# Gating unit's u half: the high and low halves of the input as one moving operand of 512 columns, with the two partial results added ahead of the Gelu

## The reference, cut to what matters

```python
def chunked_sgu_mixer(x, w_in, ln_g, ln_b, w_s, b_s, w_out):
    z = jax.nn.gelu(x @ w_in, approximate=False)
    u, v = jnp.split(z, 2, axis=-1)
    v = layer_norm(v, ln_g, ln_b)
    v = v.reshape(B, n_chunks, SGU_CHUNK, SGU_GROUPS, SGU_GROUP_DIM)
    w = jnp.where(causal[None], w_s, jnp.zeros_like(w_s))
    mixed = jnp.einsum('gts,bnsgc->bntgc', w, v) + b_s.T[None, None, :, :, None]
    return (u * mixed.reshape(B, S, SGU_HALF)) @ w_out
```

## Time and profile before

| | |
|---|---|
| median of 3 runs | 1461.29 us |
| lowest, highest | 1460.56, 1461.58 us |
| span of the profiled execution (first to last instruction) | 1459.1 us |
| mean granted TensorE clock | 0.997 |
| TensorE busy | 1440.9 us (99%) |
| VectorE busy | 1087.9 us (75%) |
| ScalarE busy | 688.2 us (47%) |
| GpSimd busy | 206.9 us (14%) |

### The profile page before, as it was taken

How to read it: one execution, slowest core, us unless ns; L and a number is a source line. 1 busy time by engine, 2 the same in 40 slices (tenths; PEclk the granted TensorE clock), 3 DMA queues, 4 the chain that set the end, 5 groups by cost and what they waited for, 6 DMA issues and landing times.

```text
span 1459.1 us, 20805 instructions
## 1 busy us (share of the span) xinstructions
PE 1440.9 (99%) x7452; PEld 1215.4 (83%) x7452; DVE 1087.9 (75%) x1825; ACT 688.2 (47%) x854; POOL 206.9 (14%) x190
## 2 busy tenths in 40 slices
PE   9999999999999999999999999999999999999997
PEld 7988897888888888889988888898888897788886
DVE  5765757888778877757758877777877777688876
ACT  6346456444444444454435444465444477444442
POOL 1073111200001000300032000301000325510001
PEclk9999999999999999999999999999999999999999
DMA  8754653855656556566567556576556450465561
GB/s 276 233 170 151 198 172 125 301 178 187 212 185 208 172 191 211 173 207 198 170 205 238 173 194 208 172 244 219 173 190 212 147 178 30 136 238 174 181 212 67
DMA packets 198734, 273.96 MB, mean 188 GB/s; under 512 B 9617, under 2 KB 158225, under 8 KB 198418
## 3 DMA queue, kind: packets, MB, share of 16 engines
q1 hardware_dynamic: 194162, 256.10, 53.2%
q0 software_dynamic: 4368, 16.78, 3.3%
q10 hardware_dynamic: 144, 0.26, 0.0%
HBM read 271.80 MB, written 1.31 MB: 187 GB/s over the span
## 4 chain that ended last, share of the span: by engine, by line
PE 90%; DVE 3%; POOL 3%; ACT 2%; issue 1%; DMA 0%; SPq 0%; DVEq 0%; ACTq 0%; POOLq 0%
PE ps L665 26%; PE ps L667 25%; PE ps L666 25%; PE ps L777 3%; PE ps L760 3%; PE ps L771 3%; PE ps L706 1%; POOL wlo L2792 1%; ACT whi L1443 1%; PE ps L1151 0%; PE ps L1279 0%; DVE big L2616 0%; DMA raw<-in_w_in 0%; DVE wlo L2014 0%; POOL big L2838 0%
## 5 line engine op out<-in xcount | busy, mean ns | idle before, releaser
L2014 DVE TENSOR_TENSOR wlo<-raw,whi 128x2048 fp32r<-128x2048 f32 (+1 forms) x222 | 504.6, 2290 | 167.5 <-ACT whi L1443 165.5
L1443 ACT CAST whi<-raw 128x2048 fp32r<-128x2048 f32 (+1 forms) x237 | 449.0, 1894 | 372.5 <-PE ps L667 327.4
L665 PE MATMUL ps<-whi,st_hi 128*128 128x512 f32 (+1 forms) x1064 | 414.7, 390 | 0.0
L667 PE MATMUL ps<-whi,st_lo 128*128 128x512 f32 (+1 forms) x1064 | 412.5, 388 | 0.0
L666 PE MATMUL ps<-wlo,st_hi 128*128 128x512 f32 (+1 forms) x1064 | 412.3, 388 | 0.0
L2428 DVE STREAM_TRANSPOSE hidT<-hidden 32x128 f32<-32x128 f32 x800 | 242.3, 303 | 12.3
L667 PEld LDWEIGHTS ps<-whi,st_lo 128*128 128x128 f32 (+1 forms) x1064 | 198.8, 187 | 41.0
L665 PEld LDWEIGHTS ps<-whi,st_hi 128*128 128x128 f32 (+1 forms) x1064 | 198.9, 187 | 40.7 <-issue 0.3
L666 PEld LDWEIGHTS ps<-wlo,st_hi 128*128 128x128 f32 (+1 forms) x1064 | 198.9, 187 | 40.2
L665 PE MATMUL ps<-whi,hid_hi 128*128 128x512 f32 x400 | 156.2, 391 | 0.0
L667 PE MATMUL ps<-whi,hid_lo 128*128 128x512 f32 x400 | 155.7, 389 | 0.0
(11 more groups left out here) (267 smaller groups left out, 1431.9 us busy)
## 6 DMA issues: line engine op xcount, KB each, us to landing
raw<-in_ffn_w SPq DMA_DIRECT2D x260, 512.0 KB, 4.8
raw<-in_w_gate_up SPq DMA_DIRECT2D x44, 512.0 KB, 4.8
raw<-in_w_in SPq DMA_DIRECT2D x32, 512.0 KB, 5.2
raw<-in_sgu_w_in SPq DMA_DIRECT2D x32, 512.0 KB, 4.7
raw<-in_w_down SPq DMA_DIRECT2D x22, 512.0 KB, 5.2
raw<-in_sgu_w_out SPq DMA_DIRECT2D x16, 512.0 KB, 4.7
raw<-in_kv_w SPq DMA_DIRECT2D x12, 512.0 KB, 4.6
raw<-in_w_proj_attn SPq DMA_DIRECT2D x8, 512.0 KB, 4.3
```

The lines of the kernel that those rows point to most:

```text
L665: pe.matmul(o, a[0], b[0], start=start, stop=False)
L667: return pe.matmul(o, a[1], b[0], start=False, stop=stop)
L1443: act.copy(whi[:, s, 0:n], raw_unit(u, s, n)).then_inc(whi_ready, 1)
L2014: dve.tensor_tensor(wlo[:, s, 0:n], raw_unit(u, s, n), whi[:, s, 0:n].bitcast(F32), ALU.subtract).then_inc(wlo_ready, 1)
```

## The change

`st_hi` and `st_lo` become two halves of one tensor. For each unit and each block t of 128 features there is a bank of its own. The high weights are multiplied with both halves at once (two runs of 256 columns, 512 columns in all) into the two halves of the bank; the low weights are multiplied with the high input into the left half. So the left half holds high by high plus low by high, the right half high by low. ScalarE copies the right half to SBUF, VectorE adds the left half to it into `zu`, and the Gelu then works in place on `zu`. In the last of the 8 tiles the order of the two matmuls is turned. Banks are 6 and 7 for even n, 0 and 2 for odd n. VectorE's sum of unit n stands behind the low part of unit n + 2, and the sum of unit 0 ahead of `norm_v(1)`. `features` and `product` stay as they are for all other stages.

```diff
-        st_hi = sb("st_hi", [P, 16, S], F32R)
-        st_lo = sb("st_lo", [P, 16, S], F32R)
+        st_both = sb("st_both", [P, 2, 16, S], F32R)
+        st_hi, st_lo = st_both[:, 0, :, :], st_both[:, 1, :, :]
...
+        u_part = tmp[:, :, 512:512 + S]
...
-            plan(("sgu", j), 6 + n % 2, unit=first["sgu"] + n)
+            plan(("sgu", j, 0), (6, 0)[n % 2])
+            plan(("sgu", j, 1), (7, 2)[n % 2], unit=first["sgu"] + n)
...
-                key = ("sgu", j)
-                room(key)
-                features(first["sgu"] + n, [(0, bank(key)[:, 0:S]), (P, bank(key)[:, S:2 * S])]).then_inc(w_used, 1)
+                w_hi, w_lo = weights(first["sgu"] + n, KD, 256)
+                for t in range(2):
+                    key = ("sgu", j, t)
+                    room(key)
+                    both = bank(key).rearrange("p (x t) -> p x t", x=2)
+                    for k in range(KD):
+                        def high():
+                            return pe.matmul(both, w_hi[:, k, t * P:t * P + P], st_both[:, :, k, :], start=k == 0,
+                                             stop=k == KD - 1)
+                        if k < KD - 1:
+                            high()
+                        pe.matmul(both[:, 0, :], w_lo[:, k, t * P:t * P + P], st_hi[:, k, :], start=False, stop=False)
+                        if k == KD - 1:
+                            mm = high()
+                    if t == 0:
+                        mm.then_inc(*is_full(key))
+                    else:
+                        mm.then_inc(w_used, 1)
...
+            def u_low(n):
+                j = SGU_ORDER[n]
+                for t in range(2):
+                    act.wait_ge(*full(("sgu", j, t)))
+                    if n:
+                        act.wait_ge(u_ready, n)
+                    act.copy(u_part[:, t, :], bank(("sgu", j, t))[:, S:2 * S]).then_inc(u_low_copied, 1)
+
+            def u_gelu(n):
+                j = SGU_ORDER[n]
+                for t in range(2):
+                    act.wait_ge(*read(("sgu", j, t)))
+                z = zu[:, 2 * j:2 * j + 2, :].rearrange("p a b -> p (a b)")
+                act.activation(z, z, ACT.Gelu).then_inc(u_ready, 1)
+
             for n, j in enumerate(SGU_ORDER):
                 beside(first["sgu"] + n)
-                act.wait_ge(*full(("sgu", j)))
-                act.activation(zu[:, 2 * j:2 * j + 2, :].rearrange("p a b -> p (a b)"), bank(("sgu", j)),
-                               ACT.Gelu).then_inc(*is_read(("sgu", j)))
+                u_low(n)
+                u_gelu(n)
...
-                dve.wait_ge(*read(("sgu", j)))
+                dve.wait_ge(u_ready, n + 1)
...
+            def u_sum(n):
+                j = SGU_ORDER[n]
+                for t in range(2):
+                    dve.wait_ge(u_low_copied, 2 * n + t + 1)
+                    key = ("sgu", j, t)
+                    dve.tensor_tensor(zu[:, 2 * j + t, :], bank(key)[:, 0:S], u_part[:, t, :],
+                                      ALU.add).then_inc(*is_read(key))
+
             norm_v(0)
             beside(first["sgu"])
+            u_sum(0)
             norm_v(1)
             for n in range(1, 5):
                 beside(first["sgu"] + n)
+                u_sum(n)
             um_mix(0)
             um_mix(1)
             beside(first["sgu"] + 5)
+            u_sum(5)
             um_low(0)
             um_low(1)
...
```

More of the change, by code:

```diff
@@ L239, in build @@
         ws_masked = sem("ws_masked")
+        u_low_copied = sem("u_low_copied")
+        u_ready = sem("u_ready")
         u_mixed = sem("u_mixed")
@@ L2531, in _ @@
             beside(first["sgu"] + 6)
+            u_sum(6)
             um_low(2)
@@ L2536, in _ @@
             beside(first["sgu"] + 7)
+            u_sum(7)
             um_mix(6)
```

## The result

The changed kernel takes 1468.61 us (median of five runs, 1466.37 to 1468.96), against 1461.58 for the kernel before in the same comparison (1460.56 to 1463.33). The ratio is 1.0037, 95% interval 1.0026 to 1.0048: slower by 0.37%, outside the stated range and on the other side of it. Like start against like start gives 1.0036 and 1.0037.)

What follows compares the result with a forecast made beforehand. TensorE, busy 99% of the span, was taken as the bound. Units 44.38, mixes 7.09 and stall 1.39 gave 52.86 us against 53.17, 0.31 less: 1461.0 us forecast from a median of 1461.29, range 1459.5 to 1463.0.

Steps and rivals of the forecast that it cites:

- hand-over chain: ScalarE waits for VectorE's sum before Gelu and next rounding; all in time after unit 3, output matmul with 1.3 us slack.
- The clock: TensorE's granted clock: a stall of about 1.4 us should not lower it from 1.00.
- first stall: TensorE's new wait ahead of unit 3, forecast at 1.39 us where before there was none.
- The stall ahead of unit 3: TensorE waits until VectorE's sum 1 frees unit 3's bank: 1.39 us, unit 3 starting at 678.43.
- The direct gain: TensorE: three matmuls become two, 0.3600 to 0.3467 us, 128 times: 1.71 us saved, a unit 5.547 us.
- The two-run operand: The wide matmul reads two runs of 256 columns; no extra cost taken, a fresh start would be 0.0133 us each.
- the slow rate: Rival: each wide matmul takes 0.44 us in place of 0.227, 1486.9 us in all; chance 0.06.
- The additions and copies: Added per unit: two VectorE additions at 0.35 us and two ScalarE copies at 0.28, neither on the end's path.
- signs of being wrong: In the changed kernel's stage: a unit of 5.76 us or more, no wait at unit 3, or another wait besides.
- the second wait: Sign against the forecast: a TensorE wait besides the only one expected, about 1.4 us ahead of unit 3.
- The rivals: Four other outcomes: stall does not bite (0.12), fixed part remains (0.18), fast rate lost (0.06), handover dearer (0.10).
- The handover case: Rival: further waits at units 4 and the mixes of bank 3, mostly 1461.5 to 1463.5 us; chance 0.10.
- chance of 0.09 for slower: Whole kernel slower by over 0.2% (2.9 us): 0.06 for the lost fast rate plus 0.03 for dearer handover.

Runs made afterwards that it cites:

- e1_banks: The changed kernel with odd units in banks 4 and 5 and the mixes in 0, 2, 1, 3; 1463.29 us, ratio 1.000 to the kernel before.
- e3_filled: The changed kernel with four unneeded matmuls of constants in TensorE's wait ahead of the output matmul; 1465.43 us, ratio 1.0026 to the kernel before.

## Why the prediction was wrong, point by point

**The step that failed** is in the hand-over chain: "By the same pitches all arrives in time for the output matmul". It followed the data (the low products, the low weights) to that point and left out the third thing a matmul needs, its PSUM bank. The banks of units 3 and 4 and of the mixes had been walked through; those of the output product, which accumulates in banks 0 to 3, had not. The change put odd units into banks 0 and 2, and both facts stood ahead of the prediction: unit 7 is odd, and its sum stands behind a low part. An estimate: from the 705.1 at which the prediction has the second mixing bank free, VectorE takes 8.7 us to that low part (707.50 to 716.23 in the profile of the changed kernel), so it starts at about 713.8; the first half of sum 7 is done 2.20 + 0.42 us later at 716.4, and TensorE arrives at 713.3: a wait of 3.1 us. Measured: 3.39, with 3.54 us more in the stage than `e1_banks`.

**The clock** was argued for a stall of 1.4 us, and that was right: it stays at 1.00 behind 1.03, 1.16 and, in the one profile of it, 2.58 us. Behind the missed 3.39 us it fell, which adds 1.6 to 1.7 us, shown by `e3_filled`. The missed wait (3.54) and the clock (1.7) make the 5.3 us; gain and first stall cancel.

**The stall ahead of unit 3** was right in place and cause and nearly in size: forecast 1.39 us by the bank that sum 1 frees. Measured 1.03 us idle, counted from the modelled end of the last matmul; from start to start unit 3 comes 1.19 us late (680.78 for 679.36 + 0.23), and in the stage it is 53.22 - 51.95 = 1.27 us. VectorE's part came as worked out: low part at 678.01 for 675.77 + 2.28. TensorE arrived 0.27 us later than forecast (679.59 for 677.04 + 2.28), since its units took 5.63 us and not 5.547.

**The direct gain** was over-sized: 1.71 us forecast, 1.22 measured. The term is the pitch of the wide matmul beside a narrow one. Five pairs from 663.02 to 664.79 take 0.354 us each, and five from 691.39 to 693.12 take 0.346, where 0.3467 was assumed throughout. Why 128 fewer matmuls gave back 9.5 ns each and not 13.3 is open. The Trainium skill ("TensorE: Matmul & The Clock Gate", section "Back-to-back issue gap") has 2.5 ns beside the columns, by which 128 matmuls would be an estimated 0.32 us; but it gives this for an isolated matmul and says that in a stream the weight loads count too, which the prediction left out. The runs lie nearer the trace's pitch, at 9.5 ns.

**The two-run operand** costs at most the missing 4 ns a matmul, and the slow rate did not come: the step behind a wide matmul is 0.23 us. **The additions and copies**: two additions last 0.75 us and the next operation starts 0.66 to 0.68 behind the first, against 0.70 taken; two copies last 0.64 us and one 0.37, a pitch of 0.27 against 0.28. **The hand-over chain** of ScalarE behaved as worked out up to the mixes: rounds of 5.5 us on VectorE, ScalarE idle 4.3 and 4.9 us ahead of Gelu 0 and 1, no wait at unit 4 nor at the mixes. Of the prediction's own signs of being wrong one came, the second wait.

**The rivals.** The one that came true was not among them. The handover case came nearest ("further waits at units 4 and at the mixes of bank 3"), but those are the places where no wait came. The chance of 0.09 for slower was too small for another reason: the change gave a bank a later reader at several places of TensorE's queue, and a list of them, one for each `room` behind a changed bank, would have had the output product's in it.

## What to carry to other kernels

When a change moves an intermediate result to other PSUM banks, list every later user of those banks until the plan repeats, the next stage's accumulators first, and ask when the new reader frees each: here three bank numbers decide between 0.4% slower and even. A gain of ten nanoseconds on each of a hundred matmuls is lost to one stall, so the helper's queue has to be reordered in the same change. And a stall is to be priced twice if the clock falls behind it, as it did here behind 3.39 us; matmuls that nobody needs, put into it, brought that second part back, 1.6 us.

## What was not expected of the hardware

The same kernel starts in one of two ways, 2.2 us apart, on both chips it ran on: on one 13 of 31 runs of the kernel before were short and 18 long, on the other 7 and 18 of 27, with two outside. Most of the difference arises at the first two matmuls of constants (1.98 to 2.30 us, or 3.78). Why is not known. A comparison of spans from one profile each would have put 7.6 us on a change that costs 5.3.

TensorE's clock kept its upper level behind waits of 1.03, 1.16 and 2.58 us and lost it behind 3.39 us, 0.54 us after the matmuls had resumed and for 3.40 us: eight steps at about 0.43 instead of 0.227 us. One profile stands behind each of the three longer waits.

The fixed part of a rounded matmul, 13.3 ns by the pitches of equal neighbours, came to 9.5 ns when one in three was removed and the others alternated in width. Why it is not the same was not tried.
